# Latent projections and gates of the first block woven into its two attentions, modulation sums moved into the first FFN

## The reference, cut to what matters

```python
proj = rmsnorm(x, norm_mix_g) @ w_in
q_lat, kv_lat, k_rope, dq, dk, dv, gate_pre = split(proj)       # 384, 256, 32, 512, 512, 512, 2048
q = rmsnorm(q_lat) @ w_uq;  kv = rmsnorm(kv_lat) @ w_ukv        # latent (MLA) attention, 8 heads of 96
o_mla = causal_attention([q_nope, rope(q_pe)], [k_nope, rope(k_rope)], v_mla)
o1, o2 = the two causal attentions of (rope(dq), rope(dk), dv)  # 4 pairs of heads, 64 wide
o_diff = rmsnorm(o1 - lam * o2, subln_g) * (1 - lambda_init)
merged = sigmoid(g_mla) * (o_mla @ w_branch_mla) + sigmoid(g_diff) * (o_diff @ w_branch_diff)
x = x + merged @ w_out;   x = x + swiglu(rmsnorm(x));   x = rmsnorm(x)
```

## Time and profile before

| | |
|---|---|
| three runs | 2048.89 us median (2043.05 to 2051.16) |
| the profiled execution: its time / its span | 2047.24 us / 2045.2 us |
| busy in the span | PE 2001.5, PEld 1604.0, DVE 1030.8, ACT 708.8, POOL 78.0 us |
| mean granted TensorE clock | 0.975 |
| weights (SP queue) / ada pieces (POOL queue) | 311 x 512 KB / 72 x 512 KB |

### The profile page before, as it was taken

How to read it: one execution, slowest core, us unless ns; L and a number is a source line. 1 busy time by engine, 2 the same in 40 slices (tenths; PEclk the granted TensorE clock), 3 DMA queues, 4 the chain that set the end, 5 groups by cost and what they waited for, 6 DMA issues and landing times. The chain is left out here.

```text
span 2045.2 us, 25500 instructions
## 1 busy us (share of the span) xinstructions
PE 2001.5 (98%) x9134; PEld 1604.0 (78%) x9142; DVE 1030.8 (50%) x1587; ACT 708.8 (35%) x1196; POOL 78.0 (4%) x113
## 2 busy tenths in 40 slices
PE   8989999999999999999999999999999999999999
PEld 6765778887888888788888877767777878888887
DVE  6664555567656533453334335857833654333322
ACT  5223662234222222332222324435544533223221
POOL 0010000001111100000000010400000000000000
PEclk9885999999999999999999999999999999999999
DMA  5210113455776633233233332221111223232332
GB/s 191 62 62 0 52 32 115 133 164 177 222 220 204 205 102 103 77 105 101 92 99 96 104 102 83 63 62 42 42 42 42 83 82 103 92 103 92 103 103 92
DMA packets 57514, 207.11 MB, mean 101 GB/s; under 512 B 6448, under 2 KB 6576, under 8 KB 57440
## 3 DMA queue, kind: packets, MB, share of 16 engines
q1 hardware_dynamic: 46800, 167.68, 25.9%
q0 software_dynamic: 10640, 38.44, 6.1%
HBM read 203.96 MB, written 2.10 MB: 101 GB/s over the span
## 5 line engine op out<-in xcount | busy, mean ns | idle before, releaser
L1340 DVE TENSOR_TENSOR LO<-RAW,HI 128x1024 fp32r<-128x1024 f32 x311 | 381.8, 1228 | 512.7 <-ACT HI L955 511.1
L389 PE MATMUL PS<-XH,HI 128*128 128x512 f32 x1552 | 625.2, 403 | 8.0 <-DVE LO L1340 4.9
L391 PE MATMUL PS<-XH,LO 128*128 128x512 f32 x1552 | 608.3, 392 | 0.0
L390 PE MATMUL PS<-XL,HI 128*128 128x512 f32 x1552 | 607.6, 392 | 0.0
L955 ACT ACTIVATE HI<-RAW 128x1024 fp32r<-128x1024 f32 x311 | 327.9, 1056 | 586.1 <-PE PS L391 568.3
L389 PEld LDWEIGHTS PS<-XH,HI 128*128 128x128 f32 x1552 | 294.2, 190 | 82.5 <-issue 13.9
L391 PEld LDWEIGHTS PS<-XH,LO 128*128 128x128 f32 x1552 | 293.2, 189 | 62.9
L390 PEld LDWEIGHTS PS<-XL,HI 128*128 128x128 f32 x1552 | 294.2, 190 | 55.0
L389 PE MATMUL PS<-HIDH,HI 128*128 128x512 f32 x528 | 205.4, 389 | 0.0
L390 PE MATMUL PS<-HIDL,HI 128*128 128x512 f32 x528 | 205.4, 389 | 0.0
L391 PE MATMUL PS<-HIDH,LO 128*128 128x512 f32 x528 | 205.4, 389 | 0.0
(11 more groups left out here) (328 smaller groups left out, 2131.4 us busy)
## 6 DMA issues: line engine op xcount, KB each, us to landing
RAW<-weights SPq DMA_DIRECT2D x311, 512.0 KB, 3.5
ADA<-ada POOLq DMA_DIRECT2D x72, 512.0 KB, 4.6
X<-x_in SPq DMA_DIRECT2D x4, 512.0 KB, 7.0
y_out<-X SPq DMA_DIRECT2D x8, 256.0 KB, 4.6
SQC<-squares SPq DMA_DIRECT2D x1, 320.0 KB, 9.3
T<-positions POOLq DMA_DIRECT2D x1, 256.0 KB, 5.2
POS<-positions POOLq DMA_DIRECT2D x1, 256.0 KB, 3.3
LAMS<-lambdas POOLq DMA_DIRECT2D x1, 128.0 KB, 6.2
```

Source lines behind the costliest of these rows:

```text
L389: mm(bank, a, moving[0][:, t, :], start=start, stop=False)
L390: mm(bank, a, moving[1][:, t, :], start=False, stop=False)
L391: ins = mm(bank, z, moving[0][:, t, :], start=False, stop=stop)
L1340: V.tensor_tensor(LO[n0 % 3][:], RAW[n0 % 3][:], HI[n0 % 3][:].bitcast(F32), ALU.subtract)\
```

## The change

- The stream starts with dq and dk in pairs (**qk1**, 8 chunks), then dv, then the six latent chunks (**lat1**), uq, uk, uv, then 16 gate chunks (**gates1**) and 8 branch chunks.
- `project_qk1` is 8 chunks. ACT copies the products; R0 is folded into the rotary table once. `angles` and `table(0)` move to step j = 1.
- Two dv chunks are done before diff_attention, two in its steps 0 and 1. `latent_work` is a generator of 22 pieces (half a latent chunk, half a uq chunk, two outputs of uk or uv: 9 or 12 matmuls each) that diff_attention takes one or two per step. The scores use three banks instead of four, transposes and value products one bank each instead of two. Norm sums, roots, table(1), rotations of the shared key and the queries are put at named steps.
- attention(1) gets gate_blocks with a chunk per two units: two blocks before and two after the transposes of every unit. DVE copies the finished gate times R0 out of bank 7.
- The outputs are turned at the end of attention(1), then `branch(0)`, the form of the second block.
- The 72 ada pieces move: 56 to the seven loop rounds of ffn(0)'s up part (as many per round as before), 8 to its first and 8 to its last down round; `modulation` splits; ada_sum(8) takes the place of a warming matmul in norm(4). The ada transfers start after attention(1)'s scores.

```diff
-        TURN_BANKS = [4, 5, 6, 7] * 2 + [2, 7, 0, 1] * 2
+        TURN_BANKS = [2, 7, 0, 1]
+        def piece_step(p):
+            return 2 + p if p < 5 else 7 + (p - 5) // 2 if p < 15 else p - 3
+        LATENT_CHUNKS = {piece_step(2 * c): c for c in range(11)}
+        GATE_CHUNKS = {1: (FIRST["gates1"], 2, 0), 2: (FIRST["gates2"], 4, 2 * DT), 3: (FIRST["gates2"] + DT, 4, 3 * DT)}
...
@@ gpsimd
-            pool.wait_ge(sem("rotated"), 1)
+            pool.wait_ge(sem("kr_rotated"), 1)
...
+            pool.wait_ge(sem("scores"), 2 * NU)
+            for j in range(2):
+                pool.dma_start(ADA[j][:], ada[j]).then_inc(sem(f"ada{j}"), 16)
@@ tensor: diff_values, latent_work (sums, spread), diff_attention
+                if j == 0:
+                    pe.wait_ge(sem("qk_copied"), 8)
...
+                def sums(k):
+                    pe.wait_ge(sem("squared"), NTB[k + 1])
...
+                def spread(k):
+                    pe.wait_ge(sem("expanded"), k + 1)
...
+                for k, t in enumerate(("q0", "q1", "q2", "k0", "k1", "kr")):
...
+                    split_product(to, w, range(4), range(4), (XH, XL), last=False)
+                    if t == "k0":
+                        sums(1)
+                    if t == "k1":
+                        spread(1)
+                    yield
+                    used(split_product(to, w, range(4, 8), range(4, 8), (XH, XL), first=False))
+                    yield
+                for j in range(3):
...
+                        if r == 0 and j < 2:
+                            (sums, spread)[j](2)
...
                         for r in range(2):
-                            bank = PS[:, SCORE_BANKS[s % 2][r], :]
+                            if 2 * s + r >= 3:
+                                pe.wait_ge(sem("probs"), 2 * s + r - 2)
+                            bank = PS[:, (2 * s + r) % 3, :]
...
+                    if s < 2:
+                        diff_values(2 + s)
+                    if pieces:
+                        next(latent)
...                      # transposes of pair s - 2, bank 3
+                    if len(pieces) == 2:
+                        next(latent)
...                      # value product of pair s - 3, bank 4
-                        if w >= 2:
-                            pe.wait_ge(sem("onorm"), w - 1)
+                        if w:
+                            pe.wait_ge(sem("onorm"), w)
@@ attention
+                    if per == 2:
+                        blocks = (((0, 1), (2, 3)), ((4, 5), (6, 7)))[u % 2][part]
...
+                        if before + c:
+                            pe.wait_ge(sem("gate_copied"), before + c)
@@ scalar: project_qk1, diff_attention
+                for j in range(10):
+                    split_hi(n0 + j)
...
+                    if 1 <= j <= 8:
+                        act.wait_ge(sem("chunk_used"), n0 + j)
+                        A(dst, PS[:, (j - 1) % 4, :], ACT.Copy, scale=scale).then_inc(sem("qk_copied"), 1)
+                    if j == 1:
+                        table(0, TAB_A1)
...
+                    if len(earlier) == 2:
+                        latent_copies(earlier[1])
...
+                    if s in LATENT_CHUNKS:
+                        split_hi(FIRST["lat1"] + LATENT_CHUNKS[s])
+                    if s == 2:
...                      # four copies of dv
...                      # copy of the transposes, two exps
+                    if pieces:
+                        latent_copies(pieces[0])
+                    if s == 2:
+                        table(1, TAB_P1)
+                    if s in (8, 11):
+                        stds(1 if s == 8 else 2)
+                    if s in (9, 12):
...                      # high(k, t)
@@ vector: diff_attention, attention
+                    if s in (8, 11):
+                        mean_squares(1 if s == 8 else 2)
+                    if s < 2:
+                        split_lo(FIRST["dv1"] + 2 + s)
+                    if s in LATENT_CHUNKS:
+                        split_lo(FIRST["lat1"] + LATENT_CHUNKS[s])
...                      # maxima of pair s, combined of pair s - 1
+                    if s == 0:
+                        rotate_qk(7)
+                    if s == 1:
+                        angles(1, TAB_P1[:, 0, :], "freq_p")
+                    if s in (8, 11):
+                        roots_of(1 if s == 8 else 2)
+                    if s in (9, 12):
+                        latent_norm(1 if s == 9 else 2)
+                    if s == 10:
+                        shared_keys()
+                    if s == 13:
+                        rotate_shared_keys()
+                    if s in (14, 15):
+                        rotate_queries(s - 14)
...
+                    if a == 1 and u % 2 == 0 and 2 <= u <= NU:
+                        c = u // 2 - 1
+                        v.wait_ge(sem("chunk_used"), n0 + c + 1)
+                        V.tensor_tensor(gate_tile(a, c), PS[:, 7, :], R0[:], ALU.mult).then_inc(sem("gate_copied"), 1)
```

More of the change, by code:

```diff
@@ L416, in norm @@
                 norm_sums(k)
-                keep_warm(WARM[k][1])
+                if k == 4:
+                    ada_sum(8, bank=4)
+                else:
+                    keep_warm(WARM[k][1])
                 norm_spread(k)
@@ L645, in diff_attention @@
             def diff_attention():
+                latent = latent_work()
                 for s in range(NPAIR + 3):
+                    pieces = [p for p in range(22) if piece_step(p) == s]
                     if s < NPAIR:
@@ L907, in _ @@
             attention(1)
-            merge(0, OTH1, OTL1)
+            after_attention(1)
+            branch(0)
             out_proj(0, MH1, ML1)
             norm(3)
-            ada_sum(1, 7)
             ffn(0, 3)
@@ L925, in _ @@
             attention(3)
-            turn(2, (3,))
-            for f in range(4):
-                pe.wait_ge(sem("onorm"), AFTER[3] + 2 * NB * (f + 1))
-                turn(3, (f,))
-            branch2()
+            after_attention(3)
+            branch(1)
             out_proj(1, MH2, ML2)
@@ L1510, in rope, with rotate_qk, project_qk1 @@
                 link(V.tensor_tensor(T[rows, 0, :], T[rows, 0, :], tab[rows, 1, :], ALU.mult))
-            def project_in1():
-                n0 = FIRST["in1"]
-                for j in range(len(IN1) + 2):
-                    if j < len(IN1):
-                        split_lo(n0 + j)
+            def rotate_qk(k):
+                dst = QK1[k][0]
+                v.wait_ge(sem("qk_copied"), k + 1)
+                rope(dst, TAB_A1, "rot_a")
+                V.tensor_tensor(dst, T[:, 0, :], T[:, 1, :], ALU.add).then_inc(sem("qk_rotated"), 1)
+                v.wait_ge(sem("qk_rotated"), k + 1)
+            def project_qk1():
+                pos = TAB_P1[:, 0, :]
+                for j in range(10):
+                    split_lo(FIRST["qk1"] + j)
                     if j == 0:
@@ new lines, in rotate_shared_keys, with rotate_queries @@
+            def rotate_shared_keys():
+                v.wait_ge(sem(LATENT_FREE["kr"][0]), LATENT_FREE["kr"][1])
+                v.wait_ge(sem("table"), 2)
+                rope(KR[:], TAB_P1, "rot_p")
+                V.tensor_tensor(KR[:], T[:, 0, :], T[:, 1, :], ALU.add).then_inc(sem("kr_rotated"), 1)
+                v.wait_ge(sem("kr_rotated"), 1)
+            def rotate_queries(r):
+                name, count = LATENT_FREE[f"uq{4 + r}"]
+                v.wait_ge(sem(name), count)
+                rope(Y[:, r, :], TAB_P1, "rot_p")
+                for h in range(4):
+                    rows = slice(32 * h, 32 * h + 32)
+                    ins = V.tensor_tensor(QM[64:96, 4 * r + h, :], T[rows, 0, :], T[rows, 1, :], ALU.add)
+                ins.then_inc(sem("q_rotated"), 1)
+                v.wait_ge(sem("q_rotated"), r + 1)
@@ L1949, in ffn, with modulation @@
                     norm(4 + f)
-            def modulation():
-                v.wait_ge(sem("mod"), 9)
-                for s in range(3):
+                if f == 0:
+                    ada_take(8, bank=4)
+                    modulation((2,))
+            def modulation(subs):
+                v.wait_ge(sem("mod"), 9 if 2 in subs else 7)
+                for s in subs:
                     c = MOD[:, (3 * s + 1) * DT:(3 * s + 2) * DT]
@@ L1978, in _ @@
             v.wait_ge(sem("split_lo"), SPLIT_TB[1])
[L1979 to L1981 removed]
+            project_qk1()
             v.wait_ge(sem("lam_exp"), 1)
@@ L2078, in _weights @@
     chunks.append(_tile(uv))
-    chunks += _merge(w1[:, o + 1536:], a["w_branch_mla"][0], a["w_branch_diff"][0])
+    merge = _merge(w1[:, o + 1536:], a["w_branch_mla"][0], a["w_branch_diff"][0], True)
+    chunks += [c for m in range(DT) for c in merge[3 * m:3 * m + 2]] + merge[2::3]
     chunks += _tiles(a["w_out"][0])
```

790 lines of the change are left out of this document (374 added, 416 removed).

## The result

The changed kernel took **2065.7 us** (median of 7 runs, 2058.2 to 2072.2) against 2049.4 before (median of 7): ratio **1.0087**, 95% interval 1.0052 to 1.0121. That is slower by 0.9%; the prediction was 2045 with "no change" likeliest. The profiled execution took 2069.9 us, its span is 2067.9, 22.7 longer than before's 2045.2.

A forecast was written before the change was run, and what follows sets the result against it. PE, 98% busy, was taken as the bound, losing about 28 us to the clock in diff_attention. Stage ends 77.8, 222.2, 377.1 and 464.3 (before 468.6): span 2045.2 - 4.3 + 1.9 = 2042.8, time 2044.8, own range 2032 to 2057, to both rivals 2016 to 2066.

The forecast's parts named there:

- Waits bring the clock down: 6.5 more.: In diff_attention: PE's waits also lower its clock, adding 6.5 us to the 24.4 us of waits.
- later: +1.9: Behind out_proj(0): moved ada sums and the modulation behind norm(4) add a net 1.9 us.
- Its transfers now start late: nothing: ada's transfers, started later where SP's queue is half idle, cost nothing.
- chunk 4's wait: In qk1: the angle table ahead of chunk 4's hi on ACT makes PE wait 4.0 us instead of 1.6.
- the waits of steps 2, 4, 7, 8 and 11: In diff_attention: PE waits 1.8, 1.6, 2.0, 3.9 and 5.9 us for chains of other engines.
- the total of steps 12 to 18: In diff_attention: DVE binds, taking 40.1 us instead of PE's own 31.0, so 9.1 us of waits.
- The gate's bank: In attention(1): PE waits for DVE to read bank 7 behind an onorm, 0.9 and 0.5, 1.4 us a head.
- The clock gain of the weave: In diff_attention: work woven between the 64-row products regains about 28 us lost to the clock.
- The clock stays down: Slower rival: the clock falls in diff_attention's step 12 and stays, PE's 31 us become 62; 2066 us, chance 0.15.
- the counter-argument: Against the slower rival: attention(3) has the same 64-row scores, with gate blocks between, and ran at clock 1.00.
- Waits hidden: Faster rival: three quarters of diff_attention's waits and most of the gate's wait go; 2017 us, chance 0.27.
- my choice of 1.28 a switch: ACT table switches in diff_attention cost the 1.28 us load alone; the skill's 2.66 would make the sum 5.5 us higher.

The follow-up runs named there:

- Experiment 3: The changed kernel with 2, 4, 6 and 4 idle full-array products put ahead of four PE waits of diff_attention; 2048.6 us, ratio 1.0038 to the kernel before.
- Experiment 1: The changed kernel with PE's ada_sum(7) behind two(1) of down0 instead of behind two(0); 2061.1 us, ratio 1.0085 to the kernel before.
- experiment 7: The kernel before with 12 idle full-array products ahead of the PV products of each diff_attention step from step 3; 2074.8 us (one run).
- experiment 6: The changed kernel with each spread of a latent norm one piece later in PE's list; 2052.5 us, ratio 1.0058 to the kernel before.
- experiment 11: The changed kernel with seven edits: ada_sum(7), gate product, angle table, spreads, uk copies, second query rotation, first latent norm's sums; 2027.9 us, ratio 0.9907 to the kernel before.
- experiment 2: The changed kernel with 4, 7, 10 and 6 idle full-array products put ahead of four PE waits of diff_attention; 2059.1 us, ratio 1.0074 to the kernel before.
- experiment 9: The changed kernel with the second query rotation alone moved behind the last onorm of diff_attention; 2064.2 us, ratio 1.0086 to the kernel before.

## Why the prediction was wrong

The sum was too low by 20.9 us (2044.8 for the execution, 2065.7 measured), and "within half a per cent" was the wrong class.

- **The step that failed** is the last of the section on the waits: "Waits bring the clock down: 6.5 more." It measured 19.1 by the mean clock, 17.3 without the idle time inside the stretches. The prediction gives no working for the 6.5. It had priced waits of some 2 us at a stretch of 3.4 us in qk1, and did not give each of five long gaps its own. By the clock in the trace these five had 3.4, 10.2, 10.2, 6.8 and 6.8 us at half clock, 37 in all, half of it lost. Experiment 3 shows how much of it comes back with four gaps filled by idle work: 12.5 us. With 19.1 for 6.5 the forecast would have had 2057.
- **The second failed term** is "later: +1.9". It was 5.8 in one execution and 12.7 in another. The larger part of both is clock again: 30.7 and 41.0 us at half clock there, against 20.5 before, so 5.1 and 10.2 us lost, for which this term had nothing. "Its transfers now start late: nothing" was wrong too: pieces that had been spread over out_proj and ffn(0) now come eight in one down round, two buffers deep, and DVE stands for ADA 0.5 to 3.5 us in five of eight pieces. PE then waits at ada_sum(0) or ada_sum(7), for 0.33 us in one execution and 1.75 in the other. ada_sum(8) behind norm(4) ran at half clock (3.55 us for 1.84), so with what follows it that stage cost 2.1 and 3.0 instead of the 1.0 taken, as far as its upper bound of 3. Experiment 1 shows that moving one sum is no remedy.
- **What was right**: chunk 4's wait (4.0; 3.98), dv's (1.95; 1.74), the waits of steps 2, 4, 7, 8 and 11, and the total of steps 12 to 18 (9.1; 1.11 + 0.23 + 0.23 + 1.69 + 3.81 + 1.32 + 0.51 = 8.9), though their place was not: I had PE wait at PV of step 16, and most of it stood at uk2, one engine further along the same chain. The gate's bank had 1.18 a head against 1.4, a head 18.6 as forecast. branch and out_proj 87.2.
- **The clock gain of the weave** (28 us) was right in kind: experiment 7 gives 25. That it was given back was the forecast; it was given back with 11 to 13 us of clock more, in the very stage that was to keep it. A smaller miss there is PE's own work, 117 us at full clock for the 113.5 of the sum.
- **The rivals.** "The clock stays down" gave 2066, which is the time measured, and its mechanism did not occur: steps 12 to 18 do not stay at 0.50. Outside the stretches at the gaps the weave ran at 1.00, as the counter-argument said. It came down at long gaps, and in experiment 6 once behind one-column sums among short products; what decides between these and the places where it stayed up is open. "Waits hidden" fell with the rows above; experiment 11 comes nearest to it, with 11.1 us of idle time left in the stage. (Its sum has a slip: three quarters of 24.4 + 6.5 are 23, not 20. The waits as listed add up to 24.3.)
- **The table load.** In step 12 the exp's table took 1.28 us from 199.25, and the exp began at 200.55, 0.02 behind it: my choice of 1.28 a switch held, and with it the length of the gaps in steps 8 and 11. By that row the 2.66 us that the Trainium skill (ScalarE: Activation LUTs, What ACT_TABLE_LOAD costs) comes to is not paid here:

```profile
199.25 1.28 ACT L1244 ACT_TABLE_LOAD   x1
200.55 0.37 ACT L1244 ACTIVATE P<-PS,SM 128x128 f32<-128x128 f32 x1
```

## What to carry to other kernels

A gap on PE in front of dense work can have two prices, its length and the lower clock behind it, and here the second was in sum as large as the first: look for it at each gap, in the windows of the trace, and don't take one lump for all. It is not fixed, as the last section shows, so give it a range. When work is woven into a stage to fill PE, list for each step what the woven piece itself waits for, and let PE issue that product a piece later than the other engines' chain ends; two edits of PE's order (the spreads) gave more than anything on the other engines. Where two engines' lists hold the same piece, edit both at once: here each of the two steps that eased one list left the wait in place or moved it.

## What the runs showed of the hardware

A product with fp32 operands on the identity over 512 columns takes 0.87 us in two records (experiment 2: 20 records in 8.74 us), one with split operands (fp32r) 0.23 in one. So a score row with "x2" is one product.

PE at half clock for 54 us without a gap came back to 0.89 over the stage with 4 full-array products of 0.24 us a step, and to 0.94 with 12. In both the later steps are at 1.00, and the 64-row products run at full clock too.

A gap of 3.94 us came with 10.2 us at half clock and one of 5.88 with 6.8: the longer gap does not cost more. In experiment 9 the same gap of 5.9 us came with 10.2, of which PE was idle for 3.9 and worked for 6.3:

```profile
188.40:192.20 3.80, 0.00 (x0) 0.00 (x0) 1.03 (x4) 3.70 (x8) 0.00 (x0) 0.50 0.30 121
192.30:198.60 6.30, 6.29 (x19) 4.87 (x20) 3.29 (x8) 0.32 (x1) 0.00 (x0) 0.50 0.00 0
```

So count only the part of a stretch that lies behind the gap: 10.2, 9.1, 6.2 and 5.6 us for the gaps of 2.11, 3.94, 5.88 and 3.81 us in the changed kernel. The same gap is not always charged the same. In experiment 6 the one of 3.82 us has 3.4 us at half clock instead of 6.8, and a gap of 1.22 us in the second block has 3.4 in the first profile of the changed kernel (a window of 8 us over it is at 0.79) and none in the second or in before (1.00 in both). Why is open. The Trainium skill (TensorE: Matmul & The Clock Gate, HAM oscillation — how this bites in real kernels) describes a kernel in which a wait in every tile makes every tile start at the lower clock. The windows over the four gaps here and what follows them agree (0.61, 0.61, 0.72 and 0.64), though PE waits for other engines here and not for a transfer. In experiment 3, with idle products in these gaps, the stage's clock is 0.98.
